# Spatial gating stage: gating weights turned two banks later, convolution columns loaded two banks ahead into two buffers

## The chip, the core and the metric

One NeuronCore of a Trainium2 chip runs the whole program. The metric is the device time of one execution in microseconds, as the median of several runs. The engines are called as in the profile: PE (TensorE), DVE (VectorE), ACT (ScalarE), POOL (GpSimd) and SP (SyncE), which here only issues DMAs.

## What is computed

Two transformer blocks follow one another on an activation of 2048 rows by 1024 columns, float32. The first normalises the rows, multiplies them by an input matrix, and splits the result into the operands of three mixers. The stage that is changed finishes two of these:

```python
def mixer_spatial_gating(u, v, gate, ln_g, ln_b, w_s, b_s):
    u = gelu(u)
    v = layer_norm(gelu(v), ln_g, ln_b)
    v = v.reshape(bsz, seq // 128, 128, 4, 64)
    v = einsum('hij,bcjhd->bcihd', w_s, v) + b_s.T[None, None, :, :, None]
    return u * v.reshape(bsz, seq, 256) * silu(gate)

def mixer_conformer_conv(a, b, gate, conv_w, conv_b, ln_g, ln_b):
    y = depthwise_conv(a * sigmoid(b), conv_w) + conv_b
    y = layer_norm(y, ln_g, ln_b)
    return silu(y) * silu(gate)
```

The convolution itself, `gelu(u)` times the gate, and the gate of the second mixer were computed by the stage before and lie in HBM scratch (`ycv`, `ug`, `sbg`).

## The kernel before, in words

`two_block_program` builds one stage after another. Between two stages `hand_over` and `wait_all` make ACT, DVE, POOL and SP (not PE) wait until the semaphores of the stage before have reached their last values, its stores to scratch included. Float32 products are split into a high and a low part, so that each product is three matmuls (`products`, L159).

`spatial_stage` (L767) writes its order of work as one list, `work`, and each of the five engines walks that list and issues its own part of each item, in order. The list is built around 16 dense products ("mm"), each of 256 rows by 256 columns, 48 matmuls of 128x256 into one PSUM bank. The first eight make `v` of the gating, eight blocks of 256 rows (evacuated by ACT through Gelu, item "av"), the last eight the second half of the attention gate (item "cg": ACT tanh, DVE L920, SP stores it to `scg`). After each mm, `advance` (L787) puts one step of every open piece into the list. There are three kinds of piece, and `LAST` (L785) holds the number of their last step:

- "ws", once: at step 0 nothing; at step 1 PE turns the four 128x128 gating weights (L850), ACT and DVE split them into `wsh` and `wsl` (L883, L923). The load of `ws` (L988) is the first DMA that SP issues in the stage.
- "sp", for each of the eight blocks of `v`: step 0, DVE moments (`dve_moments`, L895, on the tile `mv`) and POOL's power (`pool_power`, L962, on `mrs`); step 1, DVE normalises (L912), POOL multiplies and adds gain and shift (`pool_affine`, L968 and L970); step 2, ACT and DVE split `v` into `vh` and `vl` (L888, L936), SP loads `mu` from `ug` (L1000); step 3, PE's product with the gating weights (12 matmuls of 128x128), DVE's four L943, and the store (L1003).
- "cb", for each of eight blocks of the convolution's columns: step 0, SP loads the columns into `my` (L1007) and the gate into `mg` (L1009); step 1, PE turns the columns (L866), DVE takes moments from the bank (L901) and normalises into `mc` (L912), POOL's power and affine; step 2, ACT tanh (L893), DVE L955 and L958, and the store (L1013). The piece of block i is opened behind the fifth mm and later ones.

There is one `ycol` (tile `my`), so that its next load waits until PE has turned the one before. In POOL's part of the list the first item is the split of the second half of the weights (`pool_split`, L213, `w1h` and `w1l`), which waits for the load `w1r` (L200). Banks are taken in the order of the list, in turn over all eight.

```python
        work, open_ = [], [["ws", 0, 0]]
        LAST = {"ws": 1, "sp": 3, "cb": 2}
```

Of the kernel before, what the change touches and what calls it, by code (L numbers as in the profile page):

```python
# [55 lines left out]
def two_block_program(nc, A, out, ctx, stack):  # L56
# [66 lines left out]
    ident = sb("ident", [128, 128])  # L123
# [643 lines left out]
    def spatial_stage(scope, wts, first, xh, xl):  # L767
        begin()
        s_out, w_ld, r_ld = sems("sf", 2), sem("ld0"), sem("ld1")
        u_io, g_io, y_in = sem("mu0"), sems("mg", 2), sem("my0")  # L770
# [9 lines left out]
        ws, wsh, wsl = sb("ws", [128, 4, 128], scope=scope), sb("wsh", [128, 4, 128], FR, scope), sb("wsl", [128, 4, 128], FR, scope)  # L780
        rows = {n: sb("row" + n, [128, 256], scope=scope) for n in ("ag", "ab", "cg", "cb")}
# [3 lines left out]
        LAST = {"ws": 1, "sp": 3, "cb": 2}  # L785
# [26 lines left out]
        for kind, i, step in (x for x in work if x[0] in ("sp", "cb")):  # L812
            if step == (0 if kind == "sp" else 1):
                taken[kind, i] = len(taken)
            if step == 1:
                used[kind, i] = len(used) + 1
# [3 lines left out]
        for at, item in enumerate(work):  # L820
            if item[0] == "mm":
                n_mm += 1
                n, i = item[1], 2 * item[3] + item[2]
                plan[at] = plan["bank", n, i] = bk.take(a_av.at(i + 1) if n == 0 else d_si.at(i + 1))
                wts.spent[first + n] = p_mm.at(n_mm)
            elif item == ("ws", 0, 1):
                plan[at] = bk.take(d_ws.at(1))
            elif item[0] == "sp" and item[2] == 3:
                plan[at] = bk.take(d_sp.at(4 * item[1] + 4))
            elif item[0] == "cb" and item[2] == 1:  # L830
                plan[at] = bk.take(d_nm.at(2 * used["cb", item[1]]))
            elif item[0] == "cg" or item[0] == "cb" and item[2] == 2:
                plan[at] = (t_n % 2, t_free[t_n % 2])
                t_free[t_n % 2] = d_si.at(item[1] + 1) if item[0] == "cg" else d_cb.at(2 * item[1] + 1)
                t_n += 1

        def pe_program():
            for at, item in enumerate(work):
# [6 lines left out]
                elif item == ("ws", 0, 1):  # L845
# [15 lines left out]
                elif item[0] == "cb" and item[2] == 1:  # L861
                    bank, before = plan[at]
                    pe.wait_ge(*before)
                    pe.wait_ge(*y_in.at(16 * (item[1] + 1)))
                    for q in range(4):
                        ins = nc.tensor.transpose(bank[:, 128 * q:128 * q + 128], ycol[:, q % 2, 128 * (q // 2):128 * (q // 2) + 128], ident[:])  # L866
                    ins.then_inc(*p_ct.up())

        def act_program():
            for at, item in enumerate(work):  # L870
# [10 lines left out]
                elif item == ("ws", 0, 1):  # L881
# [32 lines left out]
        def dve_program():  # L914
            for at, item in enumerate(work):
# [5 lines left out]
                elif item == ("ws", 0, 1):  # L921
# [23 lines left out]
                elif item[0] == "cb" and item[2] == 1:  # L945
# [6 lines left out]
                elif item[0] == "cb" and item[2] == 2:  # L952
# [19 lines left out]
        def pool_program():  # L972
            for item in work:
# [6 lines left out]
                elif item[0] == "cb" and item[2] == 1:  # L980
# [6 lines left out]
        def sp_program():  # L987
# [3 lines left out]
            for item in work:  # L991
# [12 lines left out]
                elif item[0] == "cb" and item[2] == 0:  # L1004
                    i = item[1]
                    sp.wait_ge(*p_ct.at(i))
                    nc.sync.dma_start(ycol[:], ycv[:, 256 * i:256 * i + 256].rearrange("(c p) s -> p c s", p=128)).then_inc(*y_in.up(16))  # L1007
                    sp.wait_ge(*g_io[i % 2].at(32 * (i // 2)))
                    nc.sync.dma_start(cgate[i % 2][:], tiles_of(sbg, i, 0, 256)).then_inc(*g_io[i % 2].up(16))  # L1009
                elif item[0] == "cb" and item[2] == 2:  # L1010
# [1294 lines left out]
```

## Time and profile before

| | us |
|---|---|
| median of 3 runs | 2494.66 (2490.2 to 2504.28) |
| profiled execution, its own time | 2501.91 |
| its span in the trace | 2500.4 |
| changed stage, first instruction behind the boundary to the first of the next | 491.72 to 609.39 |

In this execution the granted clock of PE is 0.96 over the span. PE is busy 91% of it, DVE 55%, ACT 33%, POOL 28%, and the 16 DMA engines move 123 GB/s on average. The shares are those of many stages; the argument needs the stretch of the one stage, and there what each engine waits for and who comes last. A time in the rows is counted in microseconds from the start of the span.

### The profile page before, as it was taken

The numbers are of one execution on the slowest core, as the hardware profiler recorded it, in microseconds if no ns is written. First come the engines' busy times: TensorE is split into PE (matmuls) and PEld (weight loads), VectorE is DVE, ScalarE is ACT, GpSimd is POOL, SyncE is SP. The second block draws the span as 40 slices with busy tenths as digits, with TensorE's granted clock in tenths as the row PEclk, the third lists the DMA queues.
The fourth block names the chain that finished last, engine by engine and source line by source line (L and its number), as shares of the span: only waits on it lengthen the run. The fifth ranks groups of instructions, "written<-read, shape, count | busy, mean of one in ns | idle before, by whom it ended". The sixth has DMA issues, their size and how long they took to land.

```text
span 2500.4 us, 42787 instructions
## 1 busy us (share of the span) xinstructions
PE 2271.0 (91%) x16422; PEld 2058.7 (82%) x16422; DVE 1366.4 (55%) x3442; ACT 822.2 (33%) x1918; POOL 687.8 (28%) x658
## 2 busy tenths in 40 slices
PE   6999999986886999599999999999698898996898
PEld 5988989985775887599888889889698898895776
DVE  6513968754896544752565532131486777785421
ACT  4411111111785000341122201011486676674111
POOL 0012111163322987001212121110105354653222
PEclk9999999998898999799999999999899999998999
DMA  4341320235652232322555522111767866864443
GB/s 153 97 115 60 99 90 24 68 100 161 177 120 101 85 110 102 134 82 81 177 181 174 167 77 68 51 64 47 184 147 181 191 166 163 194 185 154 151 141 108
DMA packets 283805, 308.23 MB, mean 123 GB/s; under 512 B 38113, under 2 KB 221281, under 8 KB 280145
## 3 DMA queue, kind: packets, MB, share of 16 engines
q1 hardware_dynamic: 281776, 299.46, 41.9%
q0 software_dynamic: 1680, 5.51, 0.7%
q8 instruction: 131, 2.15, 0.4%
q14 instruction: 74, 0.60, 0.1%
q10 hardware_dynamic: 144, 0.52, 0.1%
HBM read 186.95 MB, written 105.89 MB: 117 GB/s over the span
## 4 chain that ended last, share of the span: by engine, by line
PE 66%; DVE 10%; DMA 9%; issue 6%; POOL 4%; SPq 3%; ACT 2%; POOLq 0%; ACTq 0%; DVEq 0%
PE bank L165 52%; DVE bank L710 4%; DMA cm<-scr_part 4%; PE bank L1852 3%; PE bank L1853 3%; PE bank L1863 3%; DMA woR<-in_w_out 2%; PE bank L1881 2%; SPq L1972 1%; PE bank L364 1%; POOL wol L1218 1%; POOL yo L2130 1%; PE bank L1286 0%; DVE p2l L1924 0%; DMA w2r<-in_w_in 0%
## 5 line engine op out<-in xcount | busy, mean ns | idle before, releaser
L165 PE MATMUL bank<-w1h,xh 128*128 128x256 f32 (+1 forms) x896 | 257.0, 287 | 0.2
L165 PE MATMUL bank<-w1l,xh 128*128 128x256 f32 (+1 forms) x896 | 253.7, 283 | 0.0
L165 PE MATMUL bank<-w1h,xl 128*128 128x256 f32 (+1 forms) x896 | 253.5, 283 | 0.0
L165 PE MATMUL bank<-xl,w2h 128*128 128x512 f32 x640 | 249.0, 389 | 0.0
L165 PE MATMUL bank<-xh,w2h 128*128 128x512 f32 x640 | 249.0, 389 | 0.0
L165 PE MATMUL bank<-xh,w2l 128*128 128x512 f32 x640 | 249.0, 389 | 0.0
L165 PE MATMUL bank<-w2h,xh 128*128 128x256 f32 x768 | 219.0, 285 | 10.5 <-issue 9.4
L165 PE MATMUL bank<-w2l,xh 128*128 128x256 f32 x768 | 218.5, 285 | 0.0
L165 PE MATMUL bank<-w2h,xl 128*128 128x256 f32 x768 | 218.5, 284 | 0.0
L1918 DVE CUSTOM_DVE_ANT_0 s2m<-bank,mask 128x256 f32<-128x256 f32 (+1 forms) x576 | 185.9, 360 | 46.5 <-PE bank L1853 45.1
L1863 PE MATMUL bank<-ident,p2r 128*128 128x128 f32 x900 | 159.0, 290 | 42.5 <-DVE p2l L1924 42.1
L710 DVE SCALAR_TENSOR_TENSOR bank<-ain,cw,bank 128x512 f32<-128x512 f32 x240 | 181.1, 755 | 14.2 <-ACT bank L661 7.1
L1924 DVE SCALAR_TENSOR_TENSOR p2l<-bank,p2h 128x512 f16<-128x512 f32 (+1 forms) x288 | 164.9, 573 | 42.1 <-ACT p2h L1890 32.9
L165 PEld LDWEIGHTS bank<-w1h,xh 128*128 128x128 f32 x896 | 173.1, 193 | 2.7 <-issue 1.1
L165 PEld LDWEIGHTS bank<-w1l,xh 128*128 128x128 f32 x896 | 173.1, 193 | 1.3
L1890 ACT ACTIVATE p2h<-bank 128x512 f16<-128x512 f32 (+1 forms) x288 | 144.5, 502 | 87.8 <-PE bank L1863 87.1
L165 PEld LDWEIGHTS bank<-w1h,xl 128*128 128x128 f32 x896 | 173.1, 193 | 0.0
L165 PEld LDWEIGHTS bank<-w2h,xh 128*128 128x128 f32 x768 | 148.7, 194 | 11.0 <-issue 9.6
L1863 PEld LDWEIGHTS bank<-ident,p2r 128*128 128x128 f32 x900 | 108.4, 149 | 52.4 <-DVE p2l L1924 49.4
L1852 PE MATMUL bank<-qkkA,qkqA 128*128 128x256 f32 (+1 forms) x288 | 131.7, 457 | 21.3 <-DMA qklB<-scr_k2l 21.3
L165 PEld LDWEIGHTS bank<-w2l,xh 128*128 128x128 f32 x768 | 148.7, 194 | 0.1
L165 PEld LDWEIGHTS bank<-w2h,xl 128*128 128x128 f32 x768 | 148.6, 194 | 0.0
(274 smaller groups left out, 5926.5 us busy)
## 6 DMA issues: line engine op xcount, KB each, us to landing
scr_part<-ob SPq DMA_DIRECT2D x48, 264.0 KB, 2.9
cm<-scr_part SPq DMA_DIRECT2D x48, 264.0 KB, 5.1
v<-scr_v SPq DMA_DIRECT2D x12, 1040.0 KB, 8.2
w2r<-in_w_in SPq DMA_DIRECT2D x12, 1024.0 KB, 6.6
qr<-qf SPq DMA_DIRECT2D x192, 64.0 KB, 2.0
ax<-in_x SPq DMA_DIRECT2D x16, 512.0 KB, 6.2
xr<-in_x SPq DMA_DIRECT2D x16, 512.0 KB, 4.6
bx<-scr_x SPq DMA_DIRECT2D x16, 512.0 KB, 6.7
```

The costliest lines, as they stand in the source:

```text
L165: ins = nc.tensor.matmul(dst, x, y, start=k == 0 and m == 0, stop=k == n - 1 and m == 2)
L364: ins = nc.tensor.transpose(bank[:, 128 * t:128 * t + 128], xs[t][:, 128 * k:128 * k + 128], ident[:])
L710: nc.vector.scalar_tensor_tensor(total[:], ain[:, 512 * q + m:512 * q + m + 512], cw[:, c, m:m + 1], total[:], ALU.mult, ALU.add).then_inc ...
L1218: nc.gpsimd.tensor_tensor(wo.lo[:, :, wo.cols(c)], wo.raw[0][:], f(wo.hi[:, :, wo.cols(c)]), ALU.subtract).then_inc(*g_w.up())
L1852: nc.tensor.matmul(dst, buf[hh][:, qc], buf[2 + hh][:, kc], start=True, stop=False)
L1853: ins = nc.tensor.matmul(dst, buf[hh][:, qc], buf[4 + hh][:, kc], start=False, stop=True)
L1863: ins = nc.tensor.transpose(bank[:, w * hh + 128 * c:w * hh + 128 * c + 128], p[:, hh, 128 * c:128 * c + 128], ident[:])
L1881: ins = nc.tensor.matmul(bank[:, c0:c0 + n], a[:, pc], vt[:, x["v0"] + c, vc], start=c == 0 and m == 0, stop=c == nk - 1 and m == 2)
L1890: nc.scalar.activation(pth[u % 3][:, 0:2 * x["w"]], x["t"][0][:, 0:2 * x["w"]], ACT.Copy, scale=PSCALE).then_inc(*a_ph.up())
L1918: nc.vector.tensor_tensor_reduce(sm[u % 3][:, hh, 0:w], x["s"][0][:, 256 * hh:256 * hh + w], mask2[:, 256 - w:256], 1.0, -NEG, ALU.add, AL ...
L1924: nc.vector.scalar_tensor_tensor(ptl[u % 3][:, 0:w], x["t"][0][:, 0:w], PSCALE, pth[u % 3][:, 0:w], ALU.mult, ALU.subtract).then_inc(*d_pl ...
L1972: nc.sync.dma_start(f(buf[hh][half, cols]), (q2h, q2l)[hh ^ (part_ // 2)][rows, cols]).then_inc(*done.up(16))
```

## The change

The gating weights are turned at step 3 of their piece instead of step 1, that is behind the fourth mm instead of the second. The column pieces get one step more: the column load stays at step 0, the load of the gate (`mg`) moves to step 1, and PE's turn, moments and normalising to step 2, tanh and store to step 3. Everything from the turn on thus stands one mm later than before. The second buffer of the columns is `ws`, whose first content is spent when the gating weights have been turned; block i uses buffer i % 2, and its load waits for the turn of block i - 2. Lines behind L781 carry numbers higher by one or two, from L1006 on by up to six.

```diff
-        u_io, g_io, y_in = sem("mu0"), sems("mg", 2), sem("my0")
+        u_io, g_io, y_in = sem("mu0"), sems("mg", 2), sems("my", 2)
...
+        ycols = ycol[:], ws[:].rearrange("p (c h) j -> p c (h j)", c=2)
...
-        LAST = {"ws": 1, "sp": 3, "cb": 2}
+        LAST = {"ws": 3, "sp": 3, "cb": 3}
...
-                elif item == ("ws", 0, 1):
+                elif item == ("ws", 0, 3):
                     bank, before = plan[at]
                     pe.wait_ge(*before)
                     pe.wait_ge(*w_ld.at(16))
...
-                elif item[0] == "cb" and item[2] == 1:
+                elif item[0] == "cb" and item[2] == 2:
+                    i = item[1]
                     bank, before = plan[at]
                     pe.wait_ge(*before)
-                    pe.wait_ge(*y_in.at(16 * (item[1] + 1)))
+                    pe.wait_ge(*y_in[i % 2].at(16 * (i // 2 + 1)))
                     for q in range(4):
-                        ins = nc.tensor.transpose(bank[:, 128 * q:128 * q + 128], ycol[:, q % 2, 128 * (q // 2):128 * (q // 2) + 128], ident[:])
+                        ins = nc.tensor.transpose(bank[:, 128 * q:128 * q + 128], ycols[i % 2][:, q % 2, 128 * (q // 2):128 * (q // 2) + 128], ident[:])
...
                 elif item[0] == "cb" and item[2] == 0:
                     i = item[1]
-                    sp.wait_ge(*p_ct.at(i))
-                    nc.sync.dma_start(ycol[:], ycv[:, 256 * i:256 * i + 256].rearrange("(c p) s -> p c s", p=128)).then_inc(*y_in.up(16))
+                    sp.wait_ge(*p_ct.at(i - 1))
+                    if i == 1:
+                        sp.wait_ge(*p_wt.at(1))
+                    nc.sync.dma_start(ycols[i % 2], ycv[:, 256 * i:256 * i + 256].rearrange("(c p) s -> p c s", p=128)).then_inc(*y_in[i % 2].up(16))
+                elif item[0] == "cb" and item[2] == 1:
+                    i = item[1]
                     sp.wait_ge(*g_io[i % 2].at(32 * (i // 2)))
                     nc.sync.dma_start(cgate[i % 2][:], tiles_of(sbg, i, 0, 256)).then_inc(*g_io[i % 2].up(16))
-                elif item[0] == "cb" and item[2] == 2:
+                elif item[0] == "cb" and item[2] == 3:
```

The same step numbers (1 to 2, 2 to 3, and 1 to 3 of "ws") change in the parts of ACT, DVE and POOL and in the planning of banks and small tiles; those lines are left out.

Two places of the new order matter. The first is DVE's order from the third group of L943 in the stage to the fourth, before (`mv` is a block of the gating, `bank` in L901 and `mc` belong to a block of the columns):

```order
L943 SCALAR_TENSOR_TENSOR mu<-bank,bs,mu 128x2x64 x4
L936 TENSOR_TENSOR mvl<-mv,mvh 128x512
L912 TENSOR_SCALAR mv<-mv,mmv,mrs 128x256 x2
L901 BN_STATS mst<-bank 128x6 x2
L904 BN_AGGR mmv<-mst 128x2 x2
L906 TENSOR_SCALAR mrs<-mmv 128x2
L912 TENSOR_SCALAR mc<-bank,mmv,mrs 128x256 x2
L901 BN_STATS mst<-mv 128x6 x2
L904 BN_AGGR mmv<-mst 128x2 x2
L906 TENSOR_SCALAR mrs<-mmv 128x2
L943 SCALAR_TENSOR_TENSOR mu<-bank,bs,mu 128x2x64 x4
L936 TENSOR_TENSOR mvl<-mv,mvh 128x512
```

and DVE's order now, from the fourth group of L943 (L945 now; L901 is now L903, L912 L914, L936 L938):

```order
L945 SCALAR_TENSOR_TENSOR mu<-bank,bs,mu 128x2x64 x4
L938 TENSOR_TENSOR mvl<-mv,mvh 128x512
L903 BN_STATS mst<-bank 128x6 x2
L906 BN_AGGR mmv<-mst 128x2 x2
L908 TENSOR_SCALAR mrs<-mmv 128x2
L914 TENSOR_SCALAR mc<-bank,mmv,mrs 128x256 x2
L914 TENSOR_SCALAR mv<-mv,mmv,mrs 128x256 x2
L903 BN_STATS mst<-mv 128x6 x2
L906 BN_AGGR mmv<-mst 128x2 x2
L908 TENSOR_SCALAR mrs<-mmv 128x2
L945 SCALAR_TENSOR_TENSOR mu<-bank,bs,mu 128x2x64 x4
L957 SCALAR_TENSOR_TENSOR mc<-s5st,mc 128x512
```

The first column block's moments stood behind the third group and ahead of the fourth; now they stand behind the fourth, and its normalising is followed at once by that of a block of the gating. Before, the two normalisings (`mv` and `mc`) stood in the other order.

The second is SP's queue between the fourth store of `mu` and the fifth, before:

```order
L1003 DMA scr_yab<-mu 128x2x256
L1000 DMA mu<-scr_ug 128x2x256
L1013 DMA scr_yab<-mg 128x2x256
L1007 DMA my<-scr_ycv 128x2x256
L1009 DMA mg<-scr_sbg 128x2x256
L1003 DMA scr_yab<-mu 128x2x256
```

and now:

```order
L1005 DMA scr_yab<-mu 128x2x256
L1002 DMA mu<-scr_ug 128x2x256
L1015 DMA mg<-scr_sbg 128x2x256
L1011 DMA my<-scr_ycv 128x2x256
L1005 DMA scr_yab<-mu 128x2x256
L1019 DMA scr_yab<-mg 128x2x256
L1002 DMA mu<-scr_ug 128x2x256
L1015 DMA mg<-scr_sbg 128x2x256
```

The column load no longer stands behind the store of a gated column block of the same round (L1013, now L1019); the load of the gate stands one round after its columns.

## Rows read from the trace of the kernel before

**Rows 1.** The page, its head: the span of the profiled execution.
```profile
span 2500.4 us, 42787 instructions
```

**Rows 2.** Chain that ended last, end of the stage: start us, us, what.
```profile
589.96 3.44 DMA my<-scr_ycv
...
605.71 0.60 ACT s5st L880
...
607.05 2.16 DMA scr_scg<-s5s
```

**Rows 3.** Waits, 480 to 625 us: who waited for whom: total us, times, longest.
```profile
POOL w1h L217 <- DMA w1r<-in_w_in: 51.3, 1, 51.3
...
PE bank L866 <- DMA my<-scr_ycv: 9.7, 6, 2.5
```

**Rows 4.** Timeline of PE, 489 to 498 us: start, us, engine, line, operation [idle before].
```profile
488.98 0.28 PE L165 MATMUL bank<-w1l,xh 128*128 128x256 f32 x1
489.10 0.28 PE L165 MATMUL bank<-w1h,xl 128*128 128x256 f32 x1
494.55 1.09 PE L850 MATMUL bank<-ident,ws 128*128 128x128 f32 x4 [5.17 <-DMA ws<-in_w_spatial]
495.29 0.56 PE L165 MATMUL bank<-w1h,xh 128*128 128x256 f32 x1
...
497.92 0.28 PE L165 MATMUL bank<-w1h,xh 128*128 128x256 f32 x1
```

**Rows 5.** One window, 494.5 to 498 us: PEclk is the granted clock.
```profile
494.50:498.00 3.50, 3.45 (x17) 3.48 (x18) 1.57 (x5) 1.09 (x2) 0.00 (x0) 0.53 0.58 118
```

**Rows 6.** Timeline of POOL, 505 to 510 us.
```profile
505.31 4.61 POOL L219 TENSOR_TENSOR w1l<-w1r,w1h 128x2048 fp32r<-128x2048 f32 x1
509.88 0.70 POOL L962 TENSOR_TENSOR mrs<-mrs,power 128x2 f32<-128x2 f32 x1
```

**Rows 7.** Timeline of PE, 515 to 540 us: first matmul of each spatial product, first transposes.
```profile
515.56 0.30 PE L165 MATMUL bank<-mvh,wsh 128*128 128x128 f32 x1 [1.66 <-issue]
...
522.74 0.22 PE L165 MATMUL bank<-mvh,wsh 128*128 128x128 f32 x1
...
529.84 0.22 PE L165 MATMUL bank<-mvh,wsh 128*128 128x128 f32 x1
...
532.99 0.64 PE L866 MATMUL bank<-ident,my 128*128 128x128 f32 x4 [1.70 <-DMA my<-scr_ycv]
...
539.22 0.22 PE L165 MATMUL bank<-mvh,wsh 128*128 128x128 f32 x1
```

**Rows 8.** Timeline of DVE, 541 to 607 us.
```profile
541.76 0.68 DVE L936 TENSOR_TENSOR mvl<-mv,mvh 128x512 fp32r<-128x512 f32 x1
542.36 0.68 DVE L955 SCALAR_TENSOR_TENSOR mc<-s5st,mc 128x512 f32<-128x512 f32 x1
...
572.36 0.69 DVE L955 SCALAR_TENSOR_TENSOR mc<-s5st,mc 128x512 f32<-128x512 f32 x1
...
589.44 0.76 DVE L901 BATCH_NORM_STATS2 mst<-bank 128x6 f32<-128x256 f32 x2
...
591.58 1.00 DVE L912 TENSOR_SCALAR mc<-bank,mmv,mrs 128x256 f32<-128x256 f32 x2 [0.89 <-POOL mrs L962]
...
595.99 0.69 DVE L955 SCALAR_TENSOR_TENSOR mc<-s5st,mc 128x512 f32<-128x512 f32 x1 [2.82 <-ACT s5st L893]
...
603.90 0.69 DVE L955 SCALAR_TENSOR_TENSOR mc<-s5st,mc 128x512 f32<-128x512 f32 x1 [2.85 <-ACT s5st L893]
...
605.24 0.68 DVE L920 SCALAR_TENSOR_TENSOR s5s<-s5st,bank 128x512 f32<-128x512 f32 x1
606.34 0.69 DVE L920 SCALAR_TENSOR_TENSOR s5s<-s5st,bank 128x512 f32<-128x512 f32 x1 [0.42 <-ACT s5st L880]
```

**Rows 9.** Timeline of POOL, 592 to 595 us.
```profile
592.65 1.27 POOL L968 TENSOR_TENSOR mc<-mc,rowcg 128x512 f32<-128x512 f32 x1 [1.19 <-DVE mc L912]
594.00 1.29 POOL L970 TENSOR_TENSOR mc<-mc,rowcb 128x512 f32<-128x512 f32 x1
```

More of the change, by code:

```diff
@@ L812, in spatial_stage @@
         for kind, i, step in (x for x in work if x[0] in ("sp", "cb")):
-            if step == (0 if kind == "sp" else 1):
+            if step == (0 if kind == "sp" else 2):
                 taken[kind, i] = len(taken)
-            if step == 1:
+            if step == (1 if kind == "sp" else 2):
                 used[kind, i] = len(used) + 1
@@ L829, in spatial_stage @@
                 plan[at] = bk.take(d_sp.at(4 * item[1] + 4))
-            elif item[0] == "cb" and item[2] == 1:
+            elif item[0] == "cb" and item[2] == 2:
                 plan[at] = bk.take(d_nm.at(2 * used["cb", item[1]]))
-            elif item[0] == "cg" or item[0] == "cb" and item[2] == 2:
+            elif item[0] == "cg" or item[0] == "cb" and item[2] == 3:
                 plan[at] = (t_n % 2, t_free[t_n % 2])
@@ L860, in pe_program @@
                     ins.then_inc(*p_sp.up())
-                elif item[0] == "cb" and item[2] == 1:
+                elif item[0] == "cb" and item[2] == 2:
+                    i = item[1]
                     bank, before = plan[at]
                     pe.wait_ge(*before)
-                    pe.wait_ge(*y_in.at(16 * (item[1] + 1)))
+                    pe.wait_ge(*y_in[i % 2].at(16 * (i // 2 + 1)))
                     for q in range(4):
-                        ins = nc.tensor.transpose(bank[:, 128 * q:128 * q + 128], ycol[:, q % 2, 128 * (q // 2):128 * (q // 2) + 128], ident[:])
+                        ins = nc.tensor.transpose(bank[:, 128 * q:128 * q + 128], ycols[i % 2][:, q % 2, 128 * (q // 2):128 * (q // 2) + 128], ident[:])
                     ins.then_inc(*p_ct.up())
@@ L944, in dve_program @@
                                                            bs[:, h:h + 1], sgate[:, :, hs], ALU.add, ALU.mult).then_inc(*d_sp.up())
-                elif item[0] == "cb" and item[2] == 1:
+                elif item[0] == "cb" and item[2] == 2:
                     i = item[1]
@@ L951, in dve_program @@
                     dve_normalise(cbuf, view, taken["cb", i])
-                elif item[0] == "cb" and item[2] == 2:
+                elif item[0] == "cb" and item[2] == 3:
                     i, t = item[1], plan[at][0]
@@ L979, in pool_program @@
                     pool_affine(vbuf[item[1] % 3], "ag", "ab", used["sp", item[1]])
-                elif item[0] == "cb" and item[2] == 1:
+                elif item[0] == "cb" and item[2] == 2:
                     pool_power(taken["cb", item[1]])
@@ L1005, in sp_program @@
                     i = item[1]
-                    sp.wait_ge(*p_ct.at(i))
-                    nc.sync.dma_start(ycol[:], ycv[:, 256 * i:256 * i + 256].rearrange("(c p) s -> p c s", p=128)).then_inc(*y_in.up(16))
+                    sp.wait_ge(*p_ct.at(i - 1))
[4 more added lines that the diff above has]
+                    i = item[1]
                     sp.wait_ge(*g_io[i % 2].at(32 * (i // 2)))
                     nc.sync.dma_start(cgate[i % 2][:], tiles_of(sbg, i, 0, 256)).then_inc(*g_io[i % 2].up(16))
-                elif item[0] == "cb" and item[2] == 2:
+                elif item[0] == "cb" and item[2] == 3:
                     i = item[1]
```

6 lines of the change are left out of this document (3 added, 3 removed).

## The prediction

> **What bounds the kernel now.** Start with the head of the page: the profiled execution spans 2500.4 us [rows 1], and its own time, 2501.91 us, lies 7.25 us above the median of 2494.66 us. The sum below is a difference against that execution, and I carry the difference over to the median. 0.5% of the median is 12.5 us, about what a measurement of this kernel can tell from no change.
>
> The second view is the chain that ended last. The stage ends with a matmul block, ACT's tanh at 605.71 and the last store at 607.05, and a column load of 3.44 us stands in it as well [rows 2]. So the chain runs through the resources that the change touches, but it names only who came last at each step. The third view, the waits of the stretch, gives the sizes: PE waited 9.7 us in six places for column loads [rows 3] and 5.17 us for the gating weights [rows 4]. These 14.9 us are all that the change aims at, 0.6% of the kernel. The same view has POOL waiting for the second half of the weights [rows 3]. The question is whether PE's waits set the end of the stage, and that is read from what PE and DVE do directly behind each.
>
> **The gating weights, turned behind four blocks instead of two.** Before, PE stops at 489.38 (last matmul 489.10 plus 0.28), turns the weights at 494.55 [rows 4], then does three blocks and reaches the first spatial product at 515.56, where it has waited 1.66 us [rows 7]. That product needs the first block of `v`, whose power on POOL starts only at 509.88, directly behind the weight split that begins at 505.31 and takes 4.61 us [rows 6]. The split stands ahead of it in POOL's part of the list, waits for a DMA, and neither moves. So the product still starts at 515.56: PE does the same five blocks sooner and waits in one piece. The sum of the two waits before is 5.17 + 1.66 = 6.83 us; now they are one wait, and longer, by the time that the low clock behind the first one cost.
>
> That time is seen: in the window behind the 5.17 us of idleness the granted clock is 0.53 [rows 5], the lower level of 1.2 GHz. Twelve matmuls go from 495.29 to 497.92, 2.63 us, where the matmuls before the wait start 0.12 us apart (488.98, 489.10) and would take 1.44 us; the four transposes take 0.74 us to the next matmul, of which I count half [rows 4]. The loss is 1.2 + 0.35, about 1.5 us. It was hidden, since PE waited again at the product. The new idle piece is 6.83 + 1.5 = 8.3 us, longer than the one that lowered the clock, and behind it there is no second wait: I expect the same 1.5 us in front of everything that follows. Between nothing lost (the 1.66 us wait at 515.56 was followed by normal speed: 7.18 us to the next product [rows 7]) and twice the loss (3.0), I take the one that was measured behind a wait of this kind.
>
> The Trainium skill's page "TensorE: Matmul & The Clock Gate" (Part 1: The HAM clock gate) has a rule that speaks against the change here: the throttled clock is the default and only activity releases it, so gathering idleness costs. Its glossary prices the loss at the throttled time times (1 - K/N); applied to the 3.37 us from 494.55 to 497.92 at half rate [rows 4] that estimate is 1.7 us, and the sum would end 0.2 us higher. The trace agrees that a long pause lowered the clock (0.53).
>
> On DVE and ACT the weights' split moves behind the first normalising, into a hole: both then wait for POOL. I cost it at nothing. If the hole were gone, a 0.69 us operation would stand ahead of the first `mvl`.
>
> **The columns, turned and normalised one block later.** Per round PE needs 7.10 us (522.74 to 529.84, product and block [rows 7]). Before, the first columns were turned at 532.99, ahead of the fourth product [rows 7]. Now they are turned behind it. The fourth product starts at 529.84 + 7.10 + 1.5 = 538.44. From the start of the fourth product before, 539.22, to DVE free behind the `mvl` split, 542.36 [rows 7, 8], are 3.14 us, and the column moments now stand exactly there: 541.58.
>
> Now follow the loop. In the undisturbed end of the stage, moments start at 589.44, normalising at 591.58 (2.14 us with POOL's power between), POOL's affine at 592.65 (1.07), L955 at 595.99: 6.55 us in all [rows 8, 9]. In the stretch with gating blocks a second affine of the same size (1.35 + 1.29 = 2.64 us [rows 9]) stands on POOL, then ACT's copy to `mvh` with its hand-over (0.70, as from the end of the affine at 595.29 to L955 at 595.99 [rows 8, 9]), then `mvl` (0.60, from 541.76 to 542.36 [rows 8]), and behind `mvl` the next moments. In the new order one lap from moments to moments is 2.14 + 1.07 + 2.64 + 0.02 + 2.64 + 0.02 + 0.70 + 0.60 = 9.83 us (0.02 for each hand-over on POOL). Before, L955 went from 542.36 to 572.36 in three such laps, 10.0 each [rows 8]; there are still three, since a gating block stands between column blocks in as many rounds. Then the fourth L955 falls at 541.58 + 3 x 9.83 + 6.55 = 577.62, against 572.36: 5.3 us later. What follows is the same loop without gating blocks, L955 to L955 in 7.88 us on average (572.36 to 603.90, four laps [rows 8]), and PE is not in it. So the eighth L955 comes 5.3 us later too, at 609.2.
>
> **The end.** Before, the last L920 waited for PE's last block and ACT, 2.44 us behind the last L955 (603.90 to 606.34). Now PE is done earlier (below), and L920 follows as soon as L955 and L958 are through, as the one before it did: 1.34 us (603.90 to 605.24) [rows 8]. That gives 1.1 us back. The stage ends 5.3 - 1.1 = 4.2 us later, and the next stage, whose loads wait for the boundary, with it.
>
> **What the column loads bring.** The six waits of 9.7 us on PE go, nearly all: a load is issued a round ahead, and no longer behind the store of the block before. But they are not on the loop. In the last four rounds PE has turned the columns while DVE still waits for tanh (2.82 and 2.85 us of idleness ahead of L955 [rows 8]), and moments stand behind L955 in DVE's order. I cost the loads at nothing on the end; PE simply finishes its blocks sooner, by 9.7 us less the 1.5 us and the wait of its products for DVE. One queue remains: the load of `mg` goes a round later than its columns and still has a round before L958 needs it.
>
> **Sum:** weights 0, low clock +1.5, columns later +3.8, end -1.1: +4.2 us. 2494.66 + 4.2 = 2498.9 us (the profiled execution, 2501.91, would be 2506.1). That is 0.17% slower, within what is counted as the same. With no clock loss it is +2.7, with twice the loss +5.7; a store of `mu` that lands late ahead of the fourth gate could add another 1 to 2.
>
> **The rivals.**
>
> *PE is the bound and the waits come back* (0.03). Then 14.9 us go, 2479.8 us. For it: PE is 91% busy over the kernel and the chain that ended last names its lines. Against it: the product at 515.56 waits for POOL, and L955 for tanh. The Trainium skill's main page (Best Practices) advises to double-buffer for performance; by that alone the time would be this one. The trace disagrees as far as these rounds go.
>
> *The later place of the columns costs nothing* (0.09). If the moments of the first columns come no later on DVE than before, for instance because POOL's power finds POOL free, only the 1.1 us at the end remains: 2493.6 us. Against it: the first turn itself is 5.5 us later (532.99 against 538.44 plus its product).
>
> *The clock stays low* (0.06), the case on the other side. Between 515.56 and the fourth product PE has three rounds of 7.10 us, 21.3 us of work on the path [rows 7]. At the lower level matmuls follow at 0.219 instead of 0.12 us [rows 4], 1.8 times as long, so that a clock that stays low through all of it costs 17 us, and the end is 2.7 + 17 later: 2514.4 us. It decides by 12.5 us as soon as 9.8 us are lost, that is when about 12 us of that work run at the low level. For it: no trace here shows an idle piece of 8 us followed by dense work in this stage. Against it: behind 5.17 us the level was back in 3.4 us.
>
> *The change does not do what it says*: the column loads still stand in SP's queue behind stores of `mu` that wait for DVE, and PE still waits for some. Since they are off the loop, the time is that of the forecast, and I give it no chance of its own.
>
> **How the numbers follow.** The forecast has 0.82, its own range +1 to +9 us with the spread of a median of few runs (2490.2 to 2504.28 before). The range holds 8 in 10: 2491 to 2507. Faster by over 0.5%: 0.03, the first rival. Slower by over 0.5%: 0.06 and 0.02 for the forecast's upper tail, 0.08. The rest, 0.89, is the same.
>
> **What would show it.** In the trace of the changed kernel: PE idle for about 8.3 us in one piece ahead of the first spatial product, which starts at 515.6 when counted from a boundary at 491.7; a granted clock near 0.5 for some 3 us behind it; the first turn of columns near 540; eight L955 (L957 there), the first near 548, three laps near 9.8, four near 7.9, the last near 609; hardly a wait of PE for columns. Wrong would be a first product well ahead of 515.6, laps much shorter than 9.8, or PE's last block ending the stage.

## The result, and the profile after

| | before | after |
|---|---|---|
| median, us (20 runs each) | 2501.68 | 2509.18 |
| ratio of the runs | | 1.0029, 95% interval 1.0016 to 1.0042 |
| profiled execution, its own time | 2501.91 | 2508.42 |
| span in the trace | 2500.4 | 2506.9 |
| stage, first DMA issue to the first of the next stage | 117.67 (491.72 to 609.39) | 124.19 (492.15 to 616.34) |
| span behind the stage | 1891.0 | 1890.6 |

The change costs 0.29%, 7.3 us by the ratio and 7.5 between the medians. That lies within the half per cent counted as the same, but its interval, 4.0 to 10.5 us, excludes no change. In the traced executions the stage accounts for 6.5 us, and what follows is equal within 0.4 us. The forecast had +4.2 us. Its 2498.9 us and its range, 2491 to 2507, stood on a median of three runs, 2494.66, which 20 runs put at 2501.68; the measured 2509.18 lies 2.2 us above the range.

Below, times "behind the boundary" are counted from the stage's first DMA issue. The lines that answer to those of before: PE at the first spatial product [rows 4, 7]. The columns of this timeline are start, us, engine, line, operation [idle before]:

```profile
507.41 0.28 PE L165 MATMUL bank<-w1h,xl 128*128 128x256 f32 x1
516.01 0.45 PE L165 MATMUL bank<-mvh,wsh 128*128 128x128 f32 x1 [8.32 <-DVE mvl L938]
...
518.60 0.52 PE L165 MATMUL bank<-w1h,xh 128*128 128x256 f32 x1
```

PE does its first five blocks and the turn of the weights in one piece, stops at 507.69, and waits 8.32 us; the product starts 23.86 us behind the boundary, against 23.84 before. The wait moved and grew, as the working had it, and the product did not come sooner. Behind it the windows (busy time of PE, PEld, DVE, ACT, POOL; granted clock; DMA) read:

```profile
507.70:516.00 8.30, 0.00 (x0) 0.02 (x1) 3.41 (x10) 0.63 (x1) 6.56 (x5) 0.71 0.00 0
516.00:521.00 5.00, 4.99 (x23) 5.00 (x24) 4.02 (x14) 1.49 (x3) 3.21 (x3) 0.50 0.02 8
```

The granted clock is 0.50, the lower level, for the whole first 5 us of work: the twelve small matmuls take 2.59 us (516.01 to 518.60). From the first product to the second it is 9.60 us, against 7.18 before [rows 7], so the loss is 2.4 us and not 1.5. The waits of the stretch (total us, times, longest), against [rows 3]:

```profile
POOL w1h L217 <- DMA w1r<-in_w_in: 51.5, 1, 51.5
ACT s5st L895 <- POOL mc L972: 51.1, 8, 6.8
...
DVE mc L957 <- ACT s5st L895: 13.4, 6, 2.9
...
PE bank L165 <- DVE mvl L938: 10.5, 3, 8.3
...
PE bank L868 <- DMA ws<-scr_ycv: 1.6, 1, 1.6
```

PE's waits for columns are down from 9.7 to 1.6 us, as forecast, the wait for the gating weights is gone, and POOL still waits 51.5 us for the second half of the weights. What grew are PE's wait for `mvl` and ACT's for POOL's affine (36.5 us in the same view of before). Now DVE's timeline, to be read beside [rows 8] (L903 was L901, L914 L912, L957 L955, L922 L920):

```profile
542.95 0.76 DVE L903 BATCH_NORM_STATS2 mst<-bank 128x6 f32<-128x256 f32 x2
...
545.92 1.71 DVE L914 TENSOR_SCALAR mv<-mv,mmv,mrs 128x256 f32<-128x256 f32 x2
...
549.86 0.78 DVE L957 SCALAR_TENSOR_TENSOR mc<-s5st,mc 128x512 f32<-128x512 f32 x1
...
560.64 1.60 DVE L957 SCALAR_TENSOR_TENSOR mc<-s5st,mc 128x512 f32<-128x512 f32 x1
...
570.13 1.10 DVE L957 SCALAR_TENSOR_TENSOR mc<-s5st,mc 128x512 f32<-128x512 f32 x1 [0.28 <-ACT s5st L895]
...
580.27 0.69 DVE L957 SCALAR_TENSOR_TENSOR mc<-s5st,mc 128x512 f32<-128x512 f32 x1 [1.81 <-ACT s5st L895]
```

Moments of the first columns start at 542.95, 50.80 us behind the boundary (forecast 49.86). The fourth L957 starts at 580.27, 88.12 behind the boundary (forecast 85.90; before 80.64). Four short laps then bring the eighth:

```profile
611.80 0.69 DVE L957 SCALAR_TENSOR_TENSOR mc<-s5st,mc 128x512 f32<-128x512 f32 x1 [2.78 <-ACT s5st L895]
...
613.14 0.68 DVE L922 SCALAR_TENSOR_TENSOR s5s<-s5st,bank 128x512 f32<-128x512 f32 x1
```

611.80 - 580.27 = 31.53 us for four laps, the same 31.54 as before [rows 8]. L922 follows 1.34 us behind, as forecast, and not 2.44. The chain that ended last has lost its PE block at the end:

```profile
613.14 0.69 DVE s5s L922
613.85 2.31 DMA scr_scg<-s5s
616.34 0.69 SPq L1233
```

One lap on POOL shows what the working had not counted:

```profile
546.08 1.40 POOL L970 TENSOR_TENSOR mc<-mc,rowcg 128x512 f32<-128x512 f32 x1 [1.11 <-DVE mc L914]
547.56 1.28 POOL L972 TENSOR_TENSOR mc<-mc,rowcb 128x512 f32<-128x512 f32 x1
548.80 1.29 POOL L970 TENSOR_TENSOR mv<-mv,rowag 128x512 f32<-128x512 f32 x1
550.17 1.62 POOL L972 TENSOR_TENSOR mv<-mv,rowab 128x512 f32<-128x512 f32 x1
```

Two parts of the affines take 1.40 and 1.62 us where [rows 9] has 1.27 and 1.29. DVE at the same time (545.92 above) runs a normalising of `mv`, two instructions in 1.71 us, and L957 at 560.64 takes 1.60 us instead of 0.69. The same pair in DVE's timeline of before, ahead of POOL's affine and not under it:

```profile
543.69 0.73 DVE L912 TENSOR_SCALAR mv<-mv,mmv,mrs 128x256 f32<-128x256 f32 x2
```

The new order puts DVE work with SBUF operands under POOL's affines, and both stretch. The sign was in the trace of before, in one place: `mvl` at 551.25 takes 0.93 us there beside POOL's affine and power, and 0.68 at 541.76 [rows 8].

The three long laps of the change, read step by step beside the working's 9.83 us, are 1.3 us longer in all. In the first and the third, POOL's affine of the gating block takes 2.99 us and not 2.64 (0.7 us in both). In the second, `mvl` starts 1.19 us behind the affine's end and not 0.70, since DVE is still in the L957 of 1.60 us and the operation behind it (0.5 us). The rest is under 0.1 us.

### The profile page after: what moved, and what is told of

Its sections match the earlier page's. It is cut to its first block, busy times and chain, and to the rows that moved or that the text cites. A ratio compares the mean times of both kernels' runs of the same rounds, so it can differ in the third digit from the quotient of the medians.

```text
span 2506.9 us, 42784 instructions
## 1 busy us (share of the span) xinstructions
PE 2269.4 (91%) x16422; PEld 2057.7 (82%) x16422; DVE 1369.5 (55%) x3442; ACT 822.3 (33%) x1918; POOL 690.0 (28%) x658
## 3 DMA queue, kind: packets, MB, share of 16 engines
q1 hardware_dynamic: 281776, 299.46, 41.8%
## 4 chain that ended last, share of the span: by engine, by line
PE 64%; DVE 10%; DMA 9%; issue 6%; POOL 5%; SPq 4%; ACT 2%; POOLq 0%; DVEq 0%; ACTq 0%
PE bank L165 51%; DVE bank L710 4%; DMA cm<-scr_part 4%; PE bank L1858 3%; PE bank L1859 3%; PE bank L1869 2%; DMA woR<-in_w_out 2%; PE bank L1887 2%; SPq L1978 1%; PE bank L364 1%; POOL wol L1224 1%; POOL yo L2136 1%; DMA w1r<-in_w_in 1%; DVE p2l L1930 1%; DVE s2m L1924 1%
## 5 line engine op out<-in xcount | busy, mean ns | idle before, releaser
L165 PE MATMUL bank<-w2h,xh 128*128 128x256 f32 x768 | 219.0, 285 | 10.4 <-issue 9.3
```

Of the source, the lines that this page charges most:

```text
L165: ins = nc.tensor.matmul(dst, x, y, start=k == 0 and m == 0, stop=k == n - 1 and m == 2)
```

## The experiments

The whole kernel is a coarse scale: in the traced executions the span behind the stage was anywhere from 1879 to 1898 us with the same instructions. The stage length is the finer one and carries the verdicts; the ratio to the kernel before (12 runs or fewer against 23 to 35, for the change 20 against 20) stands beside it. Each stage length is that of one traced execution. Before and its repeat h4 agree within 0.1 us, but g1 below shows that a late load and a low clock can add 4.5 us ahead of the second product, so the time of the first product stands beside each. Of the runs with parts of the change, only h2 has a ratio whose interval excludes 1.

| run | stage, us | first product, us | first turn of columns, us | ratio (95%) |
|---|---|---|---|---|
| before / the change | 117.67 / 124.19 | 23.8 / 23.9 | 41.3 / 49.0 | 1.0029 (1.0016 to 1.0042) |
| e1 weights only | 120.61 | 24.0 | 43.8 | 1.0003 (0.9985 to 1.0021) |
| e2 columns only | 124.02 | 24.7 | 48.8 | 1.0013 (0.9995 to 1.0030) |
| e3 columns early | 120.92 | 23.8 | 41.8 | 1.0015 (0.9998 to 1.0033) |
| e4 PE busy | 122.98 | 24.1 | 46.7 | 1.0013 (0.9997 to 1.0029) |
| g1 loads only | 122.12 | 25.3 | 43.9 | 1.0006 (0.9992 to 1.0020) |
| h1 before, PE busy | 118.25 | 23.6 | 41.5 | 1.0003 (0.9988 to 1.0017) |
| h2 columns, PE busy | 124.50 | 24.4 | 48.6 | 1.0040 (1.0022 to 1.0058) |
| h3 loads, PE busy | 118.49 | 24.0 | 41.1 | 1.0005 (0.9991 to 1.0019) |
| h4 before again | 117.75 | 24.0 | 41.3 | 0.9996 (0.9978 to 1.0014) |
| f1 split later, before | 118.32 | 23.2 | 40.7 | 0.9997 (0.9977 to 1.0017) |
| f2 split later, change | 115.44 | 15.4 | 39.3 | 0.9983 (0.9963 to 1.0003) |
| f3 split later, early | 111.63 | 15.4 | 32.1 | 0.9967 (0.9950 to 0.9984) |
| f4 ACT/DVE split, early | 110.24 | 15.4 | 30.9 | 0.9956 (0.9940 to 0.9973) |
| g2 weights and split | 111.18 | 15.4 | 34.7 | 0.9977 (0.9961 to 0.9992) |
| g3 all three | 109.17 | 15.4 | 30.9 | 0.9958 (0.9941 to 0.9974) |

### Parts of the change

**e1, the weights alone.**

```diff
-        LAST = {"ws": 1, "sp": 3, "cb": 2}
+        LAST = {"ws": 3, "sp": 3, "cb": 2}
-                elif item == ("ws", 0, 1):
+                elif item == ("ws", 0, 3):
```

> Only the gating weights are turned later (behind the fourth block instead of the second), the columns are as before. The stage is counted from its first DMA issue to the first of the next stage: 117.7 us before, 124.2 us with the whole change. Theory (POOL's weight split sets the first spatial product, and the loop over DVE, POOL and ACT sets the end): the first product does not move, PE waits about 8.3 us in one piece ahead of it and loses 2.4 us to the low clock behind it, stage about 120.1 us, kernel +2.4 us. Rival (PE's waits set the end): the 5.2 us come back, stage 112.5 us.

PE waited 8.46 us in front of the first product, the second came 9.72 us behind the first, the stage took 120.61 us. The theory holds to 0.5 us, and the 112.5 us of the rival are out.

**e2, the columns alone** (the change with `"ws": 1`).

> Only the columns are changed (two buffers, loaded a round earlier than they are turned, everything from the turn on a round later), the gating weights as before. Theory: the whole change less the clock's loss of 2.4 us, stage about 121.8 us, kernel +4 us; the waits of PE for columns are gone all the same. Rival (PE's waits set the end): 9.7 us come back, stage 108 us.

124.02 us, 2.2 more than expected. The rival is out by 16 us, but the sum was not clean: the first product came 0.8 us late, and low clock behind its wait of 2.41 us cost another 1.5. Less these two the stage is 121.7 us, which is a sum and not a run, and 4.0 us over before. In the trace of before a wait of 1.66 us at that place was followed by full clock.

**e3, the change with its column pieces opened one block earlier.**

```diff
-                    if n == 0 and i >= 4 or n == 1 and i < 4:
-                        open_.append(["cb", i - 4 if n == 0 else i + 4, 0])
+                    if n == 0 and i >= 3 or n == 1 and i < 3:
+                        open_.append(["cb", i - 3 if n == 0 else i + 5, 0])
```

> The whole change, but each column piece is opened one block earlier, so that its turn stands as before behind the third product, and its load a round ahead. Theory (the late place of the turn costs, not the loads or buffers): the first moments come 6.6 us sooner than in the whole change (543.0 to 536.4 us), one more lap is a long one with a gating block in it (about 2 us), so 4 to 4.5 us sooner at the end: stage about 120 us, still above before by the clock's 2.4 us. Rival (loads or the second buffer cost): stage as with the whole change, 124 us.

120.92 us: 3.3 us of the 6.5 are undone by opening the pieces one block earlier, 0.7 less than the 4 expected, with two buffers and the load a round ahead of the turn as in the change. The rival is out.

**e4, the change with 64 extra matmuls in PE's wait.** They write into the bank of the first product, which its own first matmul starts afresh.

```diff
                     pe.wait_ge(*before)
+                    if item[1] == 0:
+                        for k in range(64):
+                            nc.tensor.matmul(bank[:, 0:256], xh[:, k % 8, 0:128], wts.hi[first % 2][:, k % 8, :], start=True, stop=True)
                     pe.wait_ge(*d_vl.at(item[1] + 1))
```

> The whole change, with 64 matmuls of 128x256 that no one reads put on PE into the bank of the first spatial product, in its wait of 8.3 us (64 x 0.12 = 7.7 us). Theory: the granted clock stays at 2.4 GHz behind the wait, the first product and the fourth come 0 and 2.4 us sooner than in the whole change, stage about 121.8 us. Rival (the loop starts late for another reason, the clock's loss is hidden): 124.2 us.

The clock stayed up; the windows of the wait and behind it:

```profile
508.00:516.00 8.00, 7.29 (x61) 7.08 (x59) 3.30 (x10) 0.63 (x1) 6.40 (x5) 1.00 0.00 0
516.00:521.00 5.00, 4.89 (x41) 4.90 (x42) 3.90 (x14) 1.30 (x3) 3.25 (x3) 1.00 0.16 54
```

The second product came 7.18 us behind the first, as before, and the columns' first turn 2.2 us sooner than in the change. But the stage was only 1.2 us shorter. DVE's timeline shows who took the rest:

```profile
540.07 1.13 DVE L948 SCALAR_TENSOR_TENSOR mu<-bank,bs,mu 128x128 f32<-128x128 f32 x4 [4.42 <-DMA mu<-scr_ug]
541.11 0.68 DVE L941 TENSOR_TENSOR mvl<-mv,mvh 128x512 fp32r<-128x512 f32 x1
541.71 0.76 DVE L906 BATCH_NORM_STATS2 mst<-bank 128x6 f32<-128x256 f32 x2
```

DVE waited 4.42 us for `mu`, because the store of the block before was issued at 533.04 and had landed 4.1 us later, when SP's queue went on to the load:

```profile
533.04 0.36 SPq L1008 DMA_DIRECT2D scr_yab<-mu  x1
537.13 0.36 SPq L1005 DMA_DIRECT2D mu<-scr_ug  x1
```

In the change the same store had landed after 2.1 us:

```profile
535.87 0.36 SPq L1005 DMA_DIRECT2D scr_yab<-mu  x1
538.01 0.36 SPq L1002 DMA_DIRECT2D mu<-scr_ug  x1
```

The single `mu` buffer, stored and loaded again, is the next thing behind the clock. As e4 ran, the clock costs the change 1.2 us net, and 5.3 us (122.98 against 117.67) are left without it. With a store as fast as that of the change, the moments of the columns would have followed the fourth product by 3.14 us as there and not by 4.22. The stage would then be 121.9 us (an estimate from these rows), the clock would be worth 2.3, and 4.2 would be left. What makes the store slower is not shown: in before and in the change, too, some stores of `mu` took 2.1 us and others 3.7 or 3.8.

**g1, the loads alone**: two buffers and a load item in the round ahead, no other operation moved.

```diff
                         open_.append(["cb", i - 4 if n == 0 else i + 4, 0])
+                        work.append(("col", open_[-1][1]))
...
-                elif item[0] == "cb" and item[2] == 0:
+                elif item[0] == "col":
                     i = item[1]
-                    sp.wait_ge(*p_ct.at(i))
+                    sp.wait_ge(*p_ct.at(i - 1))
```

> The kernel before, with nothing but the column loads changed: two buffers, each load issued a round earlier, every operation of PE, DVE, ACT and POOL in the order of before. Stage 117.7 us before. Theory (the column loads are off the loop): PE's waits for columns (9.7 us) go, the laps stay at 10.0 and 7.9 us, and only the 1.1 us between PE's last block and the last L920 come back: stage 116.6 us, kernel within 0.1% of before. Rival (PE's waits set the end): 108 us.

122.12 us, which neither theory had. The load of the second half's weights landed in 10.4 us instead of 8.9, so that the first product came 1.45 us late, and behind PE's wait of 1.96 us the clock was at or near the lower level for some 7 us:

```profile
518.00:521.00 3.00, 2.83 (x15) 2.86 (x16) 2.39 (x10) 0.60 (x1) 2.12 (x2) 0.60 0.00 0
521.00:524.00 3.00, 3.00 (x16) 3.00 (x16) 2.64 (x9) 1.23 (x2) 1.55 (x3) 0.50 0.26 90
524.00:527.00 3.00, 3.00 (x22) 3.00 (x22) 0.79 (x4) 0.00 (x0) 2.78 (x3) 0.77 0.51 175
527.00:530.00 3.00, 3.00 (x29) 3.00 (x28) 0.10 (x1) 0.04 (x1) 0.00 (x0) 1.00 0.00 0
```

The second product came 10.24 us behind the first, 3.06 us more than before. 122.12 - 1.45 - 3.06 = 117.6 us would be the stage of before, but that is a sum, not a run; hence the next four. The 1.1 us at the end that the theory had did not come back either (see h3).

**h1 to h4, the clock made equal.** 40 extra matmuls in PE's wait for the gating weights and 12 in that of the first product, in the kernel before, in e2 and in g1; and the plain kernel before once more.

> The kernel before, with 40 matmuls of 128x256 that no one reads in PE's wait for the gating weights and 12 in its wait at the first spatial product, so that no short wait there can lower the clock. Theory (in the one traced execution of before the clock's loss was hidden): first product at 23.8 us behind the boundary, stage 117 to 117.7 us as in the trace of before. Rival (the stage of before is usually longer, by low clock behind its waits): well under the stage of the plain kernel run beside it.

> The columns changed alone (two buffers, load a round ahead, turn a round later), with the same 40 and 12 matmuls, so that the clock's part is out. Theory: from the first product on this is the whole change with PE kept busy (stage 123.0 us), so 123 us, 5.3 us over before with PE kept busy, all of it from the place of the turn. Rival (the 124.0 us of the columns alone were the clock): 118 us.

> The column loads a round early alone, everything else in the order of before, with the same 40 and 12 matmuls. Theory (the 122.1 us of the loads alone were a late split and 3 us of low clock behind the 2 us wait of the first product, and the loads themselves are off the loop): 116.0 to 117 us, 0 to 1.1 us under before with PE kept busy. Rival (loads in a round of their own disturb SP's queue or the DMA engines): 120 us or more.

> The kernel before once more, for the spread of one traced execution against another: first product, granted clock behind it, stage. Theory (whether a wait of 2 us lowers the clock differs between executions): the stage lies between 117 and 121 us, and where it is over 118.5 the clock behind the first product is the lower one for some microseconds. Rival (the stage repeats to 0.5 us, and the 122.1 us of the loads alone are their own): 117.2 to 118.2 us with full clock behind the product.

The filling did not do all that it was meant to: PE, faster through its blocks, still waited 1.4 to 2.2 us at the first product and ran low behind it. But it did so alike in all three, 8.68, 8.69 and 8.69 us from first to second product, so that they can be compared. Columns a round later cost 124.50 - 118.25 = 6.3 us, or 5.5 when the 0.8 us by which the first product differs is taken off; 5.3 was expected. The 1.5 us of low clock need not reach the end alike in both orders: in h1 the first moments of columns stand only 0.5 us behind those of before. h2's `mu` also came 0.8 us late. So 5.5 is the upper of the values for the columns, and 4.0 (e2, less two terms) the lower. Loads a round earlier gave 118.49 - 118.25 = +0.2 us, -0.1 when the 0.4 us at the first product is taken off. PE's six waits for columns were worth nothing.

h3's theory had up to 1.1 us less than h1, for the end, since PE is done earlier. This did not come. In h3 the last matmul ends at 606.06, and the end of DVE's timeline reads (L962 is L955 of before, L927 is L920):

```profile
605.47 0.69 DVE L962 SCALAR_TENSOR_TENSOR mc<-s5st,mc 128x512 f32<-128x512 f32 x1 [2.85 <-ACT s5st L900]
...
606.80 1.28 DVE L927 SCALAR_TENSOR_TENSOR s5s<-s5st,bank 128x512 f32<-128x512 f32 x2
```

Two of the gate's operations still stand behind the last L955 in this order, and the stage ends 5.30 us behind it, against 5.48 in h1 and 4.54 in the change. In the change only one L922 is left there, because the last column piece itself stands one block later.

The repeat of before took 117.75 us, at full clock behind a wait of 1.86 us:

```profile
517.00:520.00 3.00, 3.00 (x27) 3.00 (x28) 2.74 (x11) 0.44 (x1) 2.44 (x2) 1.00 0.01 3
520.00:523.00 3.00, 3.00 (x27) 3.00 (x27) 2.14 (x7) 1.23 (x2) 1.55 (x3) 1.00 0.25 87
```

Here the expectation that its stage might spread up to 121 us was not met; one repeat is not enough to say how often a wait of 2 us lowers the clock, and that stays open.

### What the first product waits for

**f1, f2: POOL's split behind the first block** in the kernel before (f1) and in the change (f2).

```diff
                     advance()
+                    if n == 0 and i == 2:
+                        work.append(("split", first + 1))
...
         def pool_program():
             for item in work:
-                if item[0] == "load":
+                if item[0] == "split":
                     wts.pool_split(item[1])
```

> The kernel before, with POOL's split of the second half of the weights (6.5 us, waiting for its load until 503.3) put behind the first block's power and affine and the second block's power in POOL's order, instead of ahead of them. Theory: the first block of v is ready by about 503, but PE, which waits for the gating weights until 494.5 and then has three blocks to do, reaches the first product only at about 514: stage 117 us, 0 to 1.5 us less than before. Rival (POOL's split does not matter or its place costs later blocks): stage as before or longer.

> The whole change, with POOL's split put later in the same way. Theory: now nothing holds the first product but PE's own five blocks; it starts at about 507.5 us instead of 516.0, there is no long wait and no low clock behind it, so 8.5 + 2.4 = 10.9 us less than the whole change: stage about 113.3 us, 4 us under before. Rival (the split is late for the second half of the blocks, or the later place of the gating products on POOL costs as much): stage above 118 us.

With the weights turned early nothing moves (118.32). With the weights turned late the first product comes at 15.4 us, directly behind PE's blocks:

```profile
507.14 0.22 PE L165 MATMUL bank<-mvh,wsh 128*128 128x128 f32 x1
```

The stage is 115.44 us, 8.8 under the change and 2.2 under before; 2.1 less was gained than expected. The second block now waits for the split (second product 8.4 us behind the first and not 7.1, 1.3 us), and DVE waits for `mu` again ahead of the first column moments, which come 3.9 us behind the fourth product and not 3.1 (0.8 us). Neither edit is worth anything alone: e1 is 2.9 us over before, f1 0.7 over.

**f3, f4: with the column pieces one block earlier as well (e3's edit); f4 gives the split to ACT and DVE.** (a chunk marked `True` is one that POOL does not split; the diff is f4's).

```diff
-                chunk("n", [(AV, 256)]), chunk("n", [(CG + 256, 256)])]
+                chunk("n", [(AV, 256)]), chunk("n", [(CG + 256, 256)], True)]
...
+                if item[0] == "split":
+                    wts.act_hi(item[1])
...
+                if item[0] == "split":
+                    wts.dve_lo(item[1])
```

> The whole change with both corrections: POOL's split later, and the column pieces opened one block earlier. Theory: first product at about 507.5 us, no low clock, first moments of columns a block sooner: 4 us under the run with the split later alone, stage about 109.5 us, kernel 8 us under before. Rival (POOL becomes the bound, since all affines now crowd behind the split): stage 113 us or more.

> As the run with both corrections, but the split of the second half of the weights is done by ACT (1.9 us) and DVE (2.3 us) ahead of the fourth block's evacuation, and not by POOL (6.5 us). Theory: the first product is set by PE's five blocks in either case, so the end moves by under 1 us: stage about 109 us. Rival (POOL is the bound of the loop): the 6.5 us of POOL come back in part, stage under 107 us.

111.63 and 110.24 us. In f3, POOL's timeline has the split between the first and the second block:

```profile
502.41 1.28 POOL L972 TENSOR_TENSOR mv<-mv,rowag 128x512 f32<-128x512 f32 x1 [5.86 <-DMA rowcb<-in_conv_ln_b]
503.78 1.29 POOL L974 TENSOR_TENSOR mv<-mv,rowab 128x512 f32<-128x512 f32 x1
505.03 0.71 POOL L966 TENSOR_TENSOR mrs<-mrs,power 128x2 f32<-128x2 f32 x1
505.70 1.90 POOL L217 CAST w1h<-w1r 128x2048 fp32r<-128x2048 f32 x1
507.68 4.93 POOL L219 TENSOR_TENSOR w1l<-w1r,w1h 128x2048 fp32r<-128x2048 f32 x1
```

DVE's `mvl` and the second block's normalising ran under it, and stretched from 0.69 and 0.73 us to:

```profile
505.77 2.37 DVE L940 TENSOR_TENSOR mvl<-mv,mvh 128x512 fp32r<-128x512 f32 x1 [0.93 <-ACT mvh L892]
508.07 5.01 DVE L916 TENSOR_SCALAR mv<-mv,mmv,mrs 128x256 f32<-128x256 f32 x2
```

In f4, with nothing of it on POOL, the same two take 0.69 and 0.73 us; it is now POOL's affine under DVE's part of the split (2.28 us from 508.21) that stretches, from 1.29 us:

```profile
508.35 3.29 POOL L978 TENSOR_TENSOR mv<-mv,rowab 128x512 f32<-128x512 f32 x1
```

The second product comes 1.2 us sooner in f4, and the stage is 1.4 us shorter, not the 4.6 of the rival. In f3 POOL also waited for the gain rows' loads (5.86 us) ahead of its first affine, which no run moved.

**g2, g3: the order of before kept for the columns.** g2 is f1 with e1's edit, one buffer. g3 has e1's edit, f4's split, and g1's loads.

> The gating weights turned later and POOL's split later, the columns with one buffer and in the order of before. Theory (the gain of the runs with both corrections comes from the first product alone, not from the columns): products at 15.4, 23.7 and 30.9 us behind the boundary, first turn of columns near 33.5 us, first L955 near 43.5, then three laps of 10.0 and four of 7.9 and 5.5 us to the end: stage 110.5 us, no longer than the 111.6 us of the run that also has two buffers and the extra step. Rival (with the first product early, PE becomes the bound and the waits for columns now count): 114 us or more.

> Gating weights turned later, the second half's split done by ACT and DVE instead of POOL, and the column loads a round early into two buffers with the order of everything else as before. Theory: 1.1 us at the end and up to 2 us of PE's waits in the rounds with gating blocks less than the run with one buffer, since the laps keep the order of before: stage 107.5 to 109.5 us, the shortest of all, kernel 9 us (0.35%) under before. Rival (no room left in the loop): 110.5 us.

g2 took 111.18 us, no longer than f3 with its second buffer and extra step, and 7.1 us less than f1, from which it differs by the turn of the weights alone: that half of the change is right, once the first product no longer waits for POOL. How much of g3's further 2.0 us is the split on ACT and DVE (its second product comes 1.4 us sooner than g2's) and how much the loads is not separated. g3, at 109.17 us, is the shortest stage and beats both kernels: 2489.45 us against 2503.83, ratio 0.9958. f4's median ratio is the same within its interval, so between these two only the stage length (1.1 us) decides.

## Why the prediction failed, by its own steps

- **"The product still starts at 515.56": right** to 0.02 us, and e1, f1 and f2 show the reason given, POOL's split in front of the first power.
- **"The loss is ... about 1.5 us": undersized.** It was 2.4, with the granted clock at 0.50 for 5 us and not for 3. In e1 the loss reaches the end (2.9 us over before); e4 got back 1.2 us, and a store of `mu` that landed 1.9 us later than in the change hid the rest.
- **"Columns later +3.8": undersized**, and this is the step that failed, by the length of a lap. In the change the eighth L957 comes 7.5 us later than before (119.65 against 112.18 behind the boundary), where 5.3 was forecast; less the clock's 2.4 the columns cost 5.1 and not 3.8. Three laps from moments to moments take 30.75 us, and not 3 x 9.83 = 29.49; these 1.3 us are the operations of DVE and POOL that stretch beside each other. The working took their durations from places where they ran alone. The clock is 0.9 us ahead of the moments (50.80 against 49.86), so that the two make 2.2 of the 2.3 us that were missing in the traced execution; the rest is the end.
- **The same without the clock.** The forecast was +2.7; the change less its 2.4 us gives +4.1, and e4 measures +5.3. In e4 the moments start at 49.66 us behind the boundary, where 48.36 was forecast. Of these 1.3 us, 0.2 lie in the first product and 1.1 in the late store of `mu`, which the working named as a possible 1 to 2 and left out of the sum. Its three laps take 30.70 us.
- **"I cost the loads at nothing": right.** h3 against h1 gives +0.2 us, or -0.1 with the first product levelled.
- **"End -1.1": the number held, the reason did not.** Four laps of 7.88 and 1.34 us to the last L922 came as forecast, and the end gave back 0.95 us. But the working had it from PE being done earlier. In g3 the last matmul ends before the last L955 begins, and the stage still ends 5.36 us behind that L955 (h3 5.30, before 5.49, the change 4.54), so that PE's part is 0.1 to 0.2 us; the rest is that only one L922 stands behind the last column piece in the new order. So this term came out near by luck.
- **The base.** A further 7.0 us of the miss in the absolute time lie in the median of three runs. With +4.2 on 2501.68 the forecast would have been 2505.9, and the range, moved by the same 7.0 us, 2498 to 2514 with 2509.18 inside. The base alone, then, carried the time out of the range, and the lap and the clock account for the 2.3 us that the difference was short. The working knew the spread of 2490 to 2504 and gave it too little room.
- **The rivals.** "PE is the bound" fell with e1 and h3. "The clock stays low" did not come true: full clock was back before the second product. "The later place costs nothing" fell with e3 and h2.

## What to carry to other kernels

Before a wait is removed, ask what the waiting engine waits for next: the 5.2 us in front of the gating weights only moved in front of a product whose operand was late for a reason on another engine, and paid off (f2, g2) once that reason was gone. Moving a step a round later to give its load time costs most of the round (4.0 to 5.5 of 7.1 us here), if the step starts a loop between other engines. g3 gives the load its time and leaves the step where it was, though h3 shows no gain from the early load by itself. And where a new order puts two engines' operations side by side that before ran one after the other, their durations from the old trace no longer hold.

## What was not expected of the hardware

DVE and POOL stretched each other's float32 operations on SBUF. The normalising pair of `mv` shows it most plainly, since it stands 136 times in the stage of the 17 traces: 105 times clear of POOL's affines and weight split, at 0.73 to 0.74 us each, and 31 times under one of them, at 1.69 to 5.03 us, with nothing in between. L957 takes 0.69 us alone and up to 1.77 beside an affine, an affine 1.26 to 1.31 us alone and up to 1.63 beside L957 and its like. f3 and f4 are the experiment: where the split leaves POOL, the pair goes from 5.01 to 0.73 us. Not everything stretches. The group that writes `mu` reads a bank and one SBUF operand; it ran beside an affine or the split for over 0.5 us 91 times and never took more than 1.13 us, as alone. The normalising that reads a bank (`mc`, 1.00 us) tells nothing, since it never ran beside either.

The Trainium skill's "GPSIMD Engine Reference" (Key points) says that POOL shares its SBUF interfaces with VectorE and contends with VectorE instructions that run in a two-port mode or have two SBUF inputs. These rows agree for L957 and `mvl`, which have two SBUF inputs, and for `mu`, which has one. The `mv` pair has one SBUF input beside its two small columns and stretches all the same, so by that rule of the Trainium skill it would have to run in a two-port mode; no row here shows the mode.

Whether a short wait lowers PE's clock was not the same each time: behind waits at the first product of 1.66 and 1.86 us (before, h4) the granted clock was 1.00, behind 1.96 us (g1) it was 0.50 for at least 3 us, and behind 1.44 us (h1) it was 0.83 and then 0.60 in the two stretches of 3 us from the product on, and the second product came 1.5 us late.
